# Decoder trunk step on one core: tile 2's h2 rows in their own place, the shift adds on VectorE, and the order of the sample-attention matmuls

## The chip, the cores and the metric

The kernel runs on one core of one Trainium2 chip. The metric is the device time of one launch in microseconds. A core has TensorE (PE, with its weight loads as PEld), VectorE (DVE), ScalarE (ACT), GpSimd (POOL) and SyncE (SP), which here only starts DMAs, and 16 DMA engines that all queues share. Everything is in float32.

## What is computed

One layer for 512 prompt tokens and for 8 samples of 8 tokens each, with the same weights. The samples attend to 2048 past positions whose keys and values lie in pages of the cache.

```
h = rms_norm(x, g_pre_mix) * (1 + sc1) + sh1
z = h @ w_in                        # q, k, v, u, s
a = rms_norm(attend(q, k, v, lam), g_subln) * (1.0 - lam_init)
s_out = spatial_gating(u, vs, sgu_ws, sgu_bs, chunk_len)
mix = concat([a, s_out]) @ w_out
x = x + ga1 * rms_norm(mix, g_post_mix)
h2 = rms_norm(x, g_pre_ffn) * (1 + sc2) + sh2
f = hier_moe(h2)                    # top-1 group of 4, then top-2 of 4 experts
x = x + ga2 * rms_norm(f, g_post_ffn)
```

Each sample's attention reads 2048 keys and 2048 values of 512 numbers each. The mixture of experts has 16 experts, each with three weight matrices of 2 MB.

## The kernel before

The program is a row of stages, each written out by hand for every engine: `condition` and `project` (adaLN and the input projection), `attend_prompt`, `attend_sample`, `merge`, `experts`, `combine`. Inside a stage every engine runs its own list of instructions in the order in which the code issues them, and semaphores tie the lists together. There is no scheduler: what is written first on an engine runs first on it.

The 576 tokens lie in five tiles of rows, t = 0 to 3 with 128 prompt rows each and t = 4 with the 64 sample rows.

**The sample loop (`attend_sample`).** TensorE goes over b = 1 to 8. In pass b it issues `weights` of sample b - 1 (three parts, L1625 and L1632: it turns the softmax weights into columns), `scores` of sample b (L1597), in odd passes `logits` (L1706), then `project_half(b)` (L1679), `values` of sample b - 1 (L1647 and L1652), a turn of the sample's result (`turn_gate` L1721 in pass 1, `turn_o` L1738 after it) and a turn of a prompt tile (`mix_turn` L1663 in odd passes, `x1_turn` L1690 in even ones). `project_half(u)` is one half (512 of 1024 columns) of the prompt's output projection: tile u // 2, column half u % 2, eight matmuls of 128x512 that add up in bank 5 of PSUM. It waits for the turned tile (`mix_ev`), for its half of `w_out` (`wo_in`), and for bank 5 (`half_free`).

The cache pages come through GpSimd's own DMA queue, each sample's keys and values in two loads apiece of 2.1 MB. Keys of sample b + 2 are requested when the scores that used their place are done. Values have one pair of places for all samples but the last: in pass b GpSimd waits for the first half of `values(b - 1)` and requests the first half of sample b's values, then the same for the second:

```
for half in range(2):
    pool.wait_ge(pv_half if half == 0 else pv_done, b)
    self.load_pages(pool, self.cv, b, half, V_SLOT[half])
```

VectorE turns the keys (`turn_block`, L817), adds the position bias and takes the maximum (`bias_max`, L1455), and in even passes from 2 on makes a tile's residual sum x1 (`residual`, L1487, L1494). ScalarE takes the exponential (L1414), copies the results out of PSUM, and empties bank 5 at the start of the next pass (`take_half`, L1339, L1357). SyncE requests the second half of `w_out` at L1253 behind the column rows of the gate.

**The end of the prompt and sample part (`merge`).** VectorE makes h2 of each tile in two instructions, a scale (`h2_scale`, L1932) and the add of the shift (L1938), each over 128x1024. The tiles' rows lie in `hv[t]`. Tile 2 has tile 0's place:

```
hv = [hv0, hv1, hv0, L.at(n0 + 11456, D), L.at(n0 + 9536, D)]
```

so `h2_scale(2)` waits for the store of tile 0 to memory (`h2_out2[0]`). For tiles 2 and 3 VectorE only scales, and GpSimd adds the shift (L1899). SyncE stores the tiles in the order 0, 1, 4, 2, 3 (L1868). The sample rows' own residual and h2 are made in between (L2023, L2024, L2026, L2032; their root mean squares come over ScalarE L1339 and GpSimd L831, L832), then `route(3, 5)` picks the experts of the last two tiles (L1960 to L1981), TensorE counts ranks, and `first` finds the rows of the first expert tile. Its list goes to GpSimd, whose first gather (L2309) waits for it and for all stores of h2. From there on the experts run.

Of the kernel before, what the change touches and what calls it, by code (L numbers as in the profile page):

```python
# [29 lines left out]
NT = 5  # L30
# [188 lines left out]
class Program:  # L219
# [943 lines left out]
    def attend_sample(self, block):  # L1163
# [416 lines left out]
        def _(pe):  # L1580
# [87 lines left out]
            def project_half(u):  # L1668


                t, c = u // 2, u % 2
                pe.wait_ge(mix_ev, 2 * t + 2)
                pe.wait_ge(wo_in[c], 16)
                if u:
                    pe.wait_ge(half_free, u)
                else:
                    pe.wait_ge(own_kept, 1)
                for k in range(KC):
                    last = pe.matmul(PS[:, 5, :], mixT(t)[:, k, :], wo[c][:, k, :], start=k == 0, stop=k == KC - 1)  # L1679
                last.then_inc(half_done, 1)  # L1680
# [60 lines left out]
            for b in range(1, SB + 1):  # L1741
                f, par = b - 1, b % 2
                for part in range(3):
                    weights(f, part, 1 - par)
                if b == 1:
                    project_half(0)
                if b < SB:
                    scores(b, par)
                    if b == SB - 1:
                        pe.wait_ge(at_act, 3 * b)  # L1750
                        pe.wait_ge(wr_made, 2)
                        pe.matmul(PS[:, 4, 32:52], L.cst("ones"), w_sum, start=True, stop=True)
                    if b % 2 and b >= 3:
                        logits((b - 3) // 2)
                    project_half(b)
                values(f)
                if b == 1:
                    turn_gate()
                else:
                    turn_o(b - 2)  # L1760
                if b % 2 and b <= 5:
                    mix_turn((b + 1) // 2, b)
                if b % 2 == 0 and b <= 6:
                    x1_turn((b - 2) // 2)
            self.late_turn = x1_turn, logits, turn_o
# [11 lines left out]
    def merge(self, block):  # L1777
# [19 lines left out]
        hv = [hv0, hv1, hv0, L.at(n0 + 11456, D), L.at(n0 + 9536, D)]  # L1797
# [5 lines left out]
        scales_in, h2_shifted = self.sem("e_scales_in"), self.sem("e_h2_shifted")  # L1803
# [57 lines left out]
        def _(sp):  # L1861

            def store(t):
                if t in (2, 3):
                    sp.wait_ge(h2_shifted, t - 1)
                else:
                    sp.wait_ge(h2_done, (1, 2, 0, 0, 4)[t])
                sp.dma_start(self.h2[P * t:P * t + rows(t), :], hv[t][0:rows(t)]).then_inc(h2_out2[t % 2], 16)  # L1868
# [16 lines left out]
            for t in (0, 1, 4, 2, 3):  # L1885
                store(t)

        @block.gpsimd
        def _(pool):
# [7 lines left out]
            for t in (2, 3):  # L1897
                pool.wait_ge(h2_done, (3, 5)[t - 2])
                pool.tensor_tensor(hv[t], hv[t], shift2, ALU.add).then_inc(h2_shifted, 1)  # L1899
# [24 lines left out]
        def _(dve):  # L1924
            link = chain(dve, dchain, self.dve_count)

            def h2_scale(t, link):

                dve.wait_ge(rs2, t + 1)
                if t == 2:  # L1930
                    dve.wait_ge(h2_out2[0], 16)
                return link(dve.scalar_tensor_tensor(hv[t], self.x1[:, t, :], ss2[:, t:t + 1], scale2,  # L1932
                                                     ALU.mult, ALU.mult))

            def h2_of(t):

                h2_scale(t, link)
# [81 lines left out]
            h2_scale(2, lambda ins: ins.then_inc(h2_done, 1))  # L2019
# [6 lines left out]
            dve.tensor_tensor(x_s, x1, mod_s[1], ALU.mult).then_inc(x1_done, 1)  # L2026
            first(0, 3)
# [5 lines left out]
            h2_scale(3, lambda ins: ins.then_inc(h2_done, 1))  # L2033
# [792 lines left out]
```

## Time and profile before

| What | us |
|---|---|
| median of 3 runs (lowest, highest) | 833.25 (831.74, 834.65) |
| the profiled execution, device time | 834.4 |
| its span in the profile | 832.6 |
| PE busy in the span | 753.8 (91%) |
| DVE, ACT, POOL busy | 362.4, 184.2, 124.1 |
| mean granted clock of TensorE, share of full | 0.948 |

The page's chain of work that ended last gives PE 76%, DVE 8%, DMA 8%, issue 3%. The prompt's attention ends at about 287 us of the span, the sample loop runs from there to 468.7, `merge` to 509, the experts to about 789, `combine` to the end. Times in the rows are microseconds from the start of the span. A square bracket behind a row of the timeline says how long the engine sat idle ahead of it and what ended the idle time; "issue" there means nothing that the profile shows. A matmul of float32 is counted twice, so a group of eight reads x16. The granted clock reads 1.00 at full speed (2.4 GHz) and 0.50 at half (1.2 GHz).

### The profile page before, as it was taken

The page shows a single profiled execution, that of the slowest core. Times are in us where ns is not written, and L with a number is a line of the kernel's source. Part 1 is how long each engine was busy: PE and PEld are TensorE (multiplying, and loading weights), DVE is VectorE, ACT ScalarE, POOL GpSimd, SP SyncE. Part 2 cuts the span into 40 slices and gives each one's busy share as a digit, 9 for nine tenths or more (in the row PEclk, how much of TensorE's full clock was granted, in tenths as well). Part 3 has the DMA queues.
Part 4 walks back from the last instruction along what each step waited for, and adds up shares of the span by engine and source line. Part 5 has one row for each costly group of instructions (what it writes and reads, how often), then busy time and mean ns, then how long its engine had stood idle before and what let it go on. Part 6 is the DMA issues. An engine that isn't in the chain of part 4 may idle for free.

```text
span 832.6 us, 12324 instructions
## 1 busy us (share of the span) xinstructions
PE 753.8 (91%) x5044; PEld 363.4 (44%) x5044; DVE 362.4 (44%) x829; ACT 184.2 (22%) x427; POOL 124.1 (15%) x171
## 2 busy tenths in 40 slices
PE   4699999999999967999999854899999999999994
PEld 3144444444444543555555452444444444444431
DVE  2122343525897965868675768101221010010146
ACT  4001000124455521333333311001111011110132
POOL 2130000200000311323121321100000000000054
PEclk9699999999999988999899965999999999999997
DMA  8989085590000798999999922599999999999893
GB/s 306 407 240 419 26 353 216 155 357 26 13 2 14 286 410 347 375 414 420 408 363 404 317 107 79 197 425 400 414 416 407 426 397 410 412 401 404 372 306 114
DMA packets 36475, 249.01 MB, mean 299 GB/s; under 512 B 4137, under 2 KB 5417, under 8 KB 22978
## 3 DMA queue, kind: packets, MB, share of 16 engines
q1 hardware_dynamic: 26354, 164.49, 50.6%
q0 software_dynamic: 9120, 81.34, 25.1%
q10 hardware_dynamic: 944, 2.38, 0.8%
q8 instruction: 41, 0.67, 0.3%
q14 instruction: 16, 0.13, 0.0%
HBM read 231.79 MB, written 16.40 MB: 298 GB/s over the span
## 4 chain that ended last, share of the span: by engine, by line
PE 76%; DVE 8%; DMA 8%; issue 3%; POOL 2%; ACT 1%; SPq 1%; POOLq 0%; DVEq 0%; ACTq 0%
PE ps L778 10%; PE ps L1679 7%; PE ps L2480 7%; PE ps L2515 7%; PE ps L2490 6%; PE ps L2487 6%; PE ps L1069 5%; PE ps L1597 4%; PE ps L1647 3%; DMA sb<-in_w_ada 3%; PE ps L2520 3%; DMA h_rows<-sb 2%; PE ps L535 2%; PE ps L2452 2%; PE ps L1625 2%
## 5 line engine op out<-in xcount | busy, mean ns | idle before, releaser
L2490 PE MATMUL ps<-sb 128*128 128x512 f32 (+1 forms) x256 | 113.0, 594 | 0.0
L778 PE MATMUL ps<-sb 128*128 128x512 f32 x192 | 87.2, 609 | 1.4 <-DVE sb L436 1.4
L2414 DVE TENSOR_TENSOR sb<-sb,ps 128x512 f32<-128x512 f32 (+1 forms) x16 | 10.9, 683 | 159.9 <-PE ps L2490 79.7
L817 DVE STREAM_TRANSPOSE sb<-sb 128x1024 f32<-128x1024 f32 (+1 forms) x72 | 76.5, 1099 | 6.4 <-DMA sb<-in_cache_k,ints 6.4
L1679 PE MATMUL ps<-sb 128*128 128x512 f32 x128 | 60.8, 630 | 5.0 <-issue 5.0
L2480 PE MATMUL ps<-sb 128*128 128x512 f32 x128 | 60.6, 629 | 4.5 <-DMA sb<-in_w_gate 3.6
L1069 PE MATMUL ps<-sb 128*128 128x512 f32 x128 | 59.2, 597 | 0.3 <-DVE sb L972 0.3
L2487 PE MATMUL ps<-sb 128*64 128x512 f32 x128 | 56.6, 595 | 0.0
L778 PEld LDWEIGHTS ps<-sb 128*128 128x128 f32 x192 | 36.5, 195 | 45.8 <-issue 44.5
L2515 PE MATMUL ps<-sb 128*128 128x512 f32 x128 | 56.5, 594 | 0.0
L2490 PEld LDWEIGHTS ps<-sb 128*128 128x128 f32 (+1 forms) x256 | 41.1, 163 | 30.2 <-issue 30.1
L2309 POOL DMA_INDIRECT sb<-h_rows,ints x16 | 14.8, 928 | 232.2 <-PE ps L2452 206.1
L946 ACT ACTIVATE sb<-sb 128x128 f32<-128x128 f32 (+3 forms) x64 | 35.4, 554 | 53.7 <-DVE sb L1030 53.7
L2425 DVE COPY sb<-ps 128x512 f32<-128x512 f32 (+1 forms) x16 | 11.1, 692 | 70.7 <-PE ps L2515 49.9
L1679 PEld LDWEIGHTS ps<-sb 128*128 128x128 f32 x128 | 25.1, 203 | 37.8 <-issue 37.5
L1030 DVE CUSTOM_DVE_ANT_0 sb<-ps,sb 128x128 f32<-128x128 f32 (+3 forms) x64 | 28.7, 486 | 26.6 <-PE ps L1104 26.5
L2480 PEld LDWEIGHTS ps<-sb 128*128 128x128 f32 x128 | 25.0, 201 | 34.4 <-issue 32.8
L1597 PE MATMUL ps<-sb 32*32 32x512 f32 x1024 | 37.2, 599 | 2.1 <-issue 2.1
L2515 PEld LDWEIGHTS ps<-sb 128*128 128x128 f32 x128 | 23.7, 190 | 26.9 <-issue 26.8
L2343 ACT ACTIVATE sb<-ps 128x512 f32<-128x512 f32 (+1 forms) x16 | 9.5, 595 | 111.4 <-PE ps L2480 59.9
L1069 PEld LDWEIGHTS ps<-sb 128*128 128x128 f32 x128 | 22.9, 193 | 22.0 <-issue 20.9
L2487 PEld LDWEIGHTS ps<-sb 128*64 128x64 f32 x128 | 16.9, 137 | 32.9 <-issue 32.0
(356 smaller groups left out, 1026.0 us busy)
## 6 DMA issues: line engine op xcount, KB each, us to landing
sb<-in_w_gate SPq DMA_DIRECT2D x16, 2048.0 KB, 24.2
sb<-in_w_up SPq DMA_DIRECT2D x16, 2048.0 KB, 14.3
sb<-in_w_down SPq DMA_DIRECT2D x16, 2048.0 KB, 19.0
sb<-in_w_ada SPq DMA_DIRECT2D x12, 2048.0 KB, 18.6
sb<-in_w_in SPq DMA_DIRECT2D x5, 2048.0 KB, 22.3
sb<-in_x_prompt SPq DMA_DIRECT2D x8, 512.0 KB, 8.5
sb<-in_w_out SPq DMA_DIRECT2D x2, 2048.0 KB, 17.1
y_rows<-sb SPq DMA_DIRECT2D x8, 512.0 KB, 19.7
```

The costliest lines, as they stand in the source:

```text
L778: last = pe.matmul(PS[:, n % 4, :], L.hT[:, k, t * P:t * P + P], w[:, k, :], start=k == 0, stop=k == KC - 1)
L817: dve.transpose(block, block).then_inc(self.turned, 1)
L946: act.activation(pb[n % 3][j][:, 0:w], pb[n % 3][j][:, 0:w], ACT.Exp, bias=nm[:, q:q + 1], scale=-1.0, accum_out=sums[:, q:q + 1]).then_in ...
L1030: dve.tensor_tensor_reduce(out=pb[n % 3][j][:, 0:w], in0=PS[:, 2 * (n % 2) + j, 0:w], in1=self.dist_bias[:, h, 384 - P * i:512], scale=-1. ...
L1069: last = pe.matmul(PS[:, bank, :], L.hT[:, k, t * P:t * P + P], w[:, k, :], start=k == 0, stop=k == KC - 1)
L1597: last = pe.matmul(PS[32 * h:32 * h + 32, g, :], qst[par][r, h, 32 * c:32 * c + 32], kp[r, :, at_row:at_row + 32], start=c == 0, stop=c == 3)
L1647: last = pe.matmul(PS[c:c + 32, 7, 0:256], at[:, page, 32 * quad:32 * quad + 32], vp[:, g, 256 * quad:256 * quad + 256], start=page < 2, s ...
L1679: last = pe.matmul(PS[:, 5, :], mixT(t)[:, k, :], wo[c][:, k, :], start=k == 0, stop=k == KC - 1)
L2480: last = pe.matmul(PS[:, 0, :], x[:, k, :], w_gate[:, k, :], start=k == 0, stop=k == KC - 1)
L2487: last = pe.matmul(PS[n:P, 0, :], x[:, k, :], w_gate[:, k, :], start=k == 0, stop=k == KC - 1)
L2490: last = pe.matmul(PS[0:n, 1, :], x[:, k, :], w_up[:, k, :], start=k == 0, stop=k == KC - 1)
L2515: last = pe.matmul(PS[:, 5 + c, :], hT[:, k, :], w[:, k, 512 * c:512 * c + 512], start=k == 0, stop=k == FC - 1)
```

## The change

Four edits. Tile 2's h2 rows get a place of their own, which lies in the area of the sample scores, and the wait for tile 0's store goes. The shift adds of tiles 2 and 3 move from GpSimd to VectorE, right behind their scale; tile 3's pair moves ahead of `first(0, 3)`, where before its scale stood behind the sample rows' h2. SyncE stores the tiles in the order 0 to 4. In the sample loop `values(0)` is issued ahead of `project_half(1)`, and from pass 2 on each `project_half` is issued in two parts: its first four matmuls at the old place, its last four at the end of the pass.

```diff
-            def project_half(u):
+            def project_half(u, blocks=range(KC)):
...
-                for k in range(KC):
+                for k in blocks:
                     last = pe.matmul(PS[:, 5, :], mixT(t)[:, k, :], wo[c][:, k, :], start=k == 0, stop=k == KC - 1)
-                last.then_inc(half_done, 1)
+                if k == KC - 1:
+                    last.then_inc(half_done, 1)
...
                     if b % 2 and b >= 3:
                         logits((b - 3) // 2)
+                    if b > 1:
+                        project_half(b, range(KC // 2))
+                values(f)
+                if b == 1:
                     project_half(b)
-                values(f)
                 if b == 1:
                     turn_gate()
                 else:
...
                 if b % 2 == 0 and b <= 6:
                     x1_turn((b - 2) // 2)
+                if 1 < b < SB:
+                    project_half(b, range(KC // 2, KC))
...
-        hv = [hv0, hv1, hv0, L.at(n0 + 11456, D), L.at(n0 + 9536, D)]
+        hv = [hv0, hv1, L.at(n0 + 2560, D), L.at(n0 + 11456, D), L.at(n0 + 9536, D)]
...
-                if t in (2, 3):
-                    sp.wait_ge(h2_shifted, t - 1)
-                else:
-                    sp.wait_ge(h2_done, (1, 2, 0, 0, 4)[t])
+                sp.wait_ge(h2_done, (1, 2, 3, 4, 5)[t])
...
-            for t in (0, 1, 4, 2, 3):
+            for t in range(NT):
                 store(t)
...
-            for t in (2, 3):
-                pool.wait_ge(h2_done, (3, 5)[t - 2])
-                pool.tensor_tensor(hv[t], hv[t], shift2, ALU.add).then_inc(h2_shifted, 1)
...
-                if t == 2:
-                    dve.wait_ge(h2_out2[0], 16)
-                return link(dve.scalar_tensor_tensor(hv[t], self.x1[:, t, :], ss2[:, t:t + 1], scale2,
-                                                     ALU.mult, ALU.mult))
...
-            h2_scale(2, lambda ins: ins.then_inc(h2_done, 1))
+            h2_of(2)
             finish_logits(3)
...
             dve.tensor_tensor(x_s, x1, mod_s[1], ALU.mult).then_inc(x1_done, 1)
+            h2_of(3)
             first(0, 3)
...
             dve.scalar_tensor_tensor(hv[4][0:NS], x_s, ss2[0:NS, 4:5], mod_s[2], ALU.mult, ALU.add).then_inc(h2_done, 1)
-            h2_scale(3, lambda ins: ins.then_inc(h2_done, 1))
```

On TensorE, passes 1 to 3 of the sample loop. Before, from `scores(1)` to the turn of pass 2 (L1679 is the projection half, L1647 and L1652 are `values`):

```order
L1597 MATMUL ps<-sb 32x512 x64
L1679 MATMUL ps<-sb 128x512 x8
L1647 MATMUL ps<-sb 32x256 x32
L1652 MATMUL ps<-sb 32x256 x2
L1721 MATMUL ps<-sb 128x64 x4
L1663 MATMUL ps<-sb 128x128 x8
L1625 MATMUL ps<-sb 64x64 x32
L1632 MATMUL ps<-sb 64x64
L1597 MATMUL ps<-sb 32x512 x64
L1679 MATMUL ps<-sb 128x512 x8
L1647 MATMUL ps<-sb 32x256 x32
L1652 MATMUL ps<-sb 32x256 x2
```

The same stretch of TensorE's list with the change:

```order
L1597 MATMUL ps<-sb 32x512 x64
L1647 MATMUL ps<-sb 32x256 x32
L1652 MATMUL ps<-sb 32x256 x2
L1679 MATMUL ps<-sb 128x512 x8
L1722 MATMUL ps<-sb 128x64 x4
L1663 MATMUL ps<-sb 128x128 x8
L1625 MATMUL ps<-sb 64x64 x32
L1632 MATMUL ps<-sb 64x64
L1597 MATMUL ps<-sb 32x512 x64
L1679 MATMUL ps<-sb 128x512 x4
L1647 MATMUL ps<-sb 32x256 x32
L1652 MATMUL ps<-sb 32x256 x2
```

In pass 1 the whole projection half now stands behind `values(0)`; in pass 2 only four of its matmuls stand ahead of `values(1)`. The end of pass 2 and the start of pass 3 on TensorE, with the change (`turn_o`, `x1_turn`, the half's second part, `weights`):

```order
L1739 MATMUL ps<-sb 128x64
L1691 MATMUL ps<-sb 128x128 x8
L1679 MATMUL ps<-sb 128x512 x4
L1625 MATMUL ps<-sb 64x64 x32
L1632 MATMUL ps<-sb 64x64
```

The other four matmuls stand behind the turns, directly ahead of the next pass's `weights`, and so on up to pass 7.

On VectorE, in `merge`, from the sum of the sample rows' projection (L2016, L2017) to the first instruction of `route(3, 5)`. Before:

```order
L2017 TENSOR_TENSOR ps<-ps,sb 64x512 [waits dve_chain]
L1932 SCALAR_TENSOR_TENSOR sb<-sb 128x1024 [waits e_h2_out,f_rs2,e_summed]
L1944 SCALAR_TENSOR_TENSOR sb<-sb 128x20 [waits f_log_kept,f_rs2]
L2023 SCALAR_TENSOR_TENSOR sb<-ps,sb 64x1024 [waits f_rs1,dve_chain]
L2024 TENSOR_TENSOR sb<-sb 64x1024 [waits dve_chain]
L2026 TENSOR_TENSOR sb<-sb 64x1024 [waits e_x1]
L1990 SCALAR_TENSOR_TENSOR sb<-ps,sb 128x3 [waits e_rank]
L1992 SCALAR_TENSOR_TENSOR sb<-sb 128x384 [waits dve_chain]
L2029 TENSOR_TENSOR sb<-ps,sb 64x20 [waits f_log]
L2032 SCALAR_TENSOR_TENSOR sb<-sb 64x1024 [waits f_rs2,e_x1]
L1932 SCALAR_TENSOR_TENSOR sb<-sb 128x1024 [waits f_rs2]
L2036 SCALAR_TENSOR_TENSOR sb<-ps,sb 64x20 [waits f_log,e_log_read]
```

From the old L2026 (now L2019) on, with the change:

```order
L2019 TENSOR_TENSOR sb<-sb 64x1024
L1930 SCALAR_TENSOR_TENSOR sb<-sb 128x1024
L1931 TENSOR_TENSOR sb<-sb 128x1024
L1983 SCALAR_TENSOR_TENSOR sb<-ps,sb 128x3
L1985 SCALAR_TENSOR_TENSOR sb<-sb 128x384
L2023 TENSOR_TENSOR sb<-ps,sb 64x20
L2026 SCALAR_TENSOR_TENSOR sb<-sb 64x1024
L2029 SCALAR_TENSOR_TENSOR sb<-ps,sb 64x20
```

Tile 3's scale and add now stand between the sample rows' residual and `first(0, 3)`, and nothing stands between the sample rows' h2 (L2026 there) and the finish of their logits (L2029 there). Tile 2's pair has grown by its add in the same way, at the place of the first L1932.

## Rows read from the trace of the kernel before

**Rows 1.** Timeline of PE, pass 1: start, us, engine, line, operation, tiles, count, [idle before]

```profile
321.25 9.19 PE L1679 MATMUL ps<-sb 128*128 128x512 f32 x16 [5.04 <-issue]
330.37 3.66 PE L1647 MATMUL ps<-sb 128*32 128x256 f32 x64
334.51 0.46 PE L1721 MATMUL ps<-sb 64*128 64x64 f32 x4
```

**Rows 2.** Timeline of PE, pass 2's half, and the first `weights` of pass 3

```profile
342.44 7.21 PE L1679 MATMUL ps<-sb 128*128 128x512 f32 x16
...
355.01 2.08 PE L1625 MATMUL ps<-sb 128*64 128x64 f32 x64
```

**Rows 3.** Busy time by window (columns: PE, PEld, DVE, ACT, POOL, PEclk, DMA share, GB/s)

```profile
321.20:330.40 9.20, 9.15 (x20) 3.79 (x21) 5.02 (x7) 2.15 (x2) 0.00 (x0) 0.77 0.91 385
```

**Rows 4.** Timeline of PE, passes 4 to 6: their first `weights`, and a gap in `scores(5)`

```profile
376.55 2.09 PE L1625 MATMUL ps<-sb 128*64 128x64 f32 x64
...
395.58 2.08 PE L1625 MATMUL ps<-sb 128*64 128x64 f32 x64
...
403.44 1.48 PE L1597 MATMUL ps<-sb 32*32 32x512 f32 x8 [1.34 <-issue]
...
421.79 2.08 PE L1625 MATMUL ps<-sb 128*64 128x64 f32 x64
```

**Rows 5.** DMA: windows 330 to 335 and 385 to 395; the key load issued at 384.74

```profile
DMA packets 28, 0.36 MB, mean 72 GB/s; under 512 B 6, under 2 KB 6, under 8 KB 6
...
DMA packets 285, 4.14 MB, mean 414 GB/s; under 512 B 32, under 2 KB 32, under 8 KB 32
...
sb<-in_cache_k,ints POOLq DMA_INDIRECT x1, 14.6
```

**Rows 6.** Timeline of the loop's end and the start of `merge`, all engines

```profile
461.31 2.09 PE L1625 MATMUL ps<-sb 128*64 128x64 f32 x64
...
464.49 3.66 PE L1647 MATMUL ps<-sb 128*32 128x256 f32 x64 [0.98 <-ACT sb L1405]
...
465.63 1.23 DVE L1938 TENSOR_TENSOR sb<-sb 128x1024 f32<-128x1024 f32 x1
...
468.19 0.34 DVE L1503 SCALAR_TENSOR_TENSOR sb<-sb 64x128 f32<-64x128 f32 x1 [1.34 <-POOL sb L832]
...
468.83 3.65 PE L2145 MATMUL ps<-sb 128*64 128x512 f32 x16
...
475.53 5.35 PE L2145 MATMUL ps<-sb 128*64 128x512 f32 x16 [0.48 <-ACT sb L1383]
```

**Rows 7.** Timeline of DVE and POOL in `merge`, from the sample sum to the last ranks

```profile
481.65 0.69 DVE L2017 TENSOR_TENSOR ps<-ps,sb 64x512 f32<-64x512 f32 x1
...
487.81 1.28 DVE L1932 SCALAR_TENSOR_TENSOR sb<-sb 128x1024 f32<-128x1024 f32 x1 [5.46 <-DMA h_rows<-sb]
...
491.84 1.22 DVE L2026 TENSOR_TENSOR sb<-sb 64x1024 f32<-64x1024 f32 x1
...
493.34 0.78 POOL L832 TENSOR_TENSOR sb<-sb 64x1 f32<-64x1 f32 x1
...
494.24 3.28 DVE L2032 SCALAR_TENSOR_TENSOR sb<-sb 64x1024 f32<-64x1024 f32 x1 [0.43 <-POOL sb L832]
...
498.79 2.34 POOL L1899 TENSOR_TENSOR sb<-sb 128x1024 f32<-128x1024 f32 x1 [2.36 <-DVE sb L1932]
499.10 2.06 DVE L1960 TENSOR_TENSOR sb<-sb 128x8 f32<-128x8 f32 x1
501.19 0.17 DVE L1961 TENSOR_TENSOR sb<-sb 128x8 f32<-128x8 f32 x1
...
505.01 0.19 DVE L1981 TENSOR_TENSOR sb<-sb 128x32 f32<-128x32 f32 x1
```

**Rows 8.** The last store of h2 (issued at 501.2, us to landing) and the first gather

```profile
h_rows<-sb SPq DMA_DIRECT2D x1, 512.0 KB, 2.6
...
509.09 1.02 POOL L2309 DMA_INDIRECT sb<-h_rows,ints  x1 [7.96 <-DVE ints L2061]
```

More of the change, by code:

```diff
@@ L1802, in merge @@
         h2T = L.at(n0 + 18432, KC * NS).rearrange("p (k t) -> p k t", k=KC)
-        scales_in, h2_shifted = self.sem("e_scales_in"), self.sem("e_h2_shifted")
+        scales_in = self.sem("e_scales_in")
         st = self.stats
@@ L1925, in _, with h2_of @@
             link = chain(dve, dchain, self.dve_count)
-            def h2_scale(t, link):
+            def h2_of(t):
                 dve.wait_ge(rs2, t + 1)
-                if t == 2:
-                    dve.wait_ge(h2_out2[0], 16)
-                return link(dve.scalar_tensor_tensor(hv[t], self.x1[:, t, :], ss2[:, t:t + 1], scale2,
-                                                     ALU.mult, ALU.mult))
-            def h2_of(t):
-                h2_scale(t, link)
+                link(dve.scalar_tensor_tensor(hv[t], self.x1[:, t, :], ss2[:, t:t + 1], scale2, ALU.mult, ALU.mult))
                 dve.tensor_tensor(hv[t], hv[t], shift2, ALU.add).then_inc(h2_done, 1)
```

## The prediction

> **What bounds the kernel now.** I read the timeline of TensorE first. It is busy 91% of the span, and in the sample loop almost nothing interrupts it, so what counts there is the few places where it stands. The longest is in pass 1: `scores(1)` ends at 316.2, and the projection half starts at 321.25 after 5.04 us of idle time; it then takes 9.19 us, where the same sixteen counted matmuls take 7.21 us in pass 2 [rows 1, 2]. The window over it shows a granted clock of 0.77 instead of 1.00 [rows 3]. `values(0)`, which needs nothing of the projection, waits behind both. What ends the idle time the profile doesn't name. By the code the half waits there for ScalarE to empty bank 5 and for the second half of `w_out`, requested behind much else; ScalarE is idle by then, so I take the load.
>
> The timelines of all engines over `merge` come second. TensorE is nearly idle there and VectorE carries the chain: it sits 5.46 us until tile 0's rows are stored, because tile 2 wants their place [rows 7]. Then come tile 2's scale, the sample rows' residual, h2, the routing, and GpSimd's first gather at 509.09 [rows 8]. Behind it TensorE and the weight loads start from that gather and from lists that the same VectorE chain makes, so a microsecond won ahead of it is a microsecond of the end. The DMA windows come third. Between 385 and 395 the engines move 4.14 MB, which is two page loads of 2.1 MB, or 5.2 us for one; between 330 and 335 they are nearly idle at 72 GB/s; a key load issued at 384.74 lands 14.6 us later, behind what is queued [rows 5]. A pass needs four such loads, 20.8 us, and a pass of TensorE takes 19 to 21 us. The pages are the next bound, close below.
>
> **The merge part.** Take B as the end of the sample sum (L2017), 482.35, and A as the start of L2026. Before, A is at 491.84, or B + 9.5. The 5.46 us of waiting go. Tile 2's add comes in, one VectorE instruction of 1.23 us by the row of tile 0's add [rows 6, 7]. A is then B + 9.5 - 5.5 + 1.2 = B + 5.2, a gain of 4.2 us. Next late would be the root of the sample rows: ScalarE's square and GpSimd's two operations end near B + 2.1, and VectorE wants them at B + 2.8, so they hide.
>
> From A to the last ranks (L1981, end 505.20) there are 13.4 us before. Three things change. Tile 3's scale and add now stand ahead of `first`, 1.28 + 1.23 = 2.5 us; its scale behind L2032 goes, 1.3 us. Behind L2026 VectorE waited 0.43 us for GpSimd and L2032 took 3.28 us, against 1.22 us for L2026 of the same shape, while GpSimd added tile 2's shift; without that add beside it I take 1.2, so 2.1 + 0.4 go. The first L1960 took 2.06 us beside GpSimd's other add, while the 128x8 instruction behind it takes 0.17: 1.9 us go [rows 7]. That is -2.5 + 1.3 + 2.5 + 1.9 = 3.2 us; 0.4 us of it I don't count, for gaps and for the sample logits, which now come just in time: 2.8 us. GpSimd's root of the sample rows (0.78 us for its last operation) runs under the 2.5 us of tile 3, and the two adds leave GpSimd altogether.
>
> The moved work costs nothing elsewhere. The stores: the last was issued at 501.2 and landed in 2.6 us, 5 us ahead of the gather; now the last is tile 4's, issued some 5 us ahead of where the ranks end, and a gather still comes 3.8 us after those. The merge part gives 4.2 + 2.8 = **7.0 us**. If the cover of the two GpSimd operations is gone, it gives 6.
>
> The Trainium skill, SBUF — State Buffer, section Who interferes with whom, says that a VectorE instruction with two SBUF inputs and a GpSimd one that reads SBUF exclude each other for the whole instruction. By it the sample rows' first root, which now falls under tile 2's pair, would end near B + 3.3 and cost 0.5 us of the 7.0; the same rule is what L2032 at 3.28 us and L1960 at 2.06 us show.
>
> **Pass 1.** With `values(0)` first, TensorE works from 316.2 for the 4.1 us between its first row and the turn behind it [rows 1], to 320.4. The half still can't start before its load is there, 321.25: 0.85 us idle. Then it runs at the full clock, 7.2 instead of 9.2 us. Before, both were done at 334.5; now at 328.5. That is 6.1 us, 4.1 of overlap and 2.0 of clock.
>
> **The split halves.** They add no matmul. Values end 3.6 us earlier in each pass (half of 7.21 [rows 2]), and so GpSimd requests the next sample's value pages 3.6 us earlier, but they are also wanted 3.6 us earlier. Bank 5 is full later, at the end of the pass; ScalarE empties it in 1.4 us while `weights` and `scores` take 6.5, and x1 is wanted much later, so this hides. The scores keep their distance to the `weights` that follow.
>
> What of 6.1 us stays is up to the pages. I ran the queue forward at 5.2 us a load. It starts sample 1's values right behind the keys, which fills the nearly idle 330 to 335 and gains about 5 us on TensorE's 6. By pass 4 the second half of the values lands about 1.9 us after it is wanted. If a gap like the one in pass 5 comes again, TensorE waits no more after that. So the loop gives 6.1 - 1.9 = **4.2 us** up to here, with bounds of 0 (the pages give nothing) and 9 (that gap doesn't come again: pass 5 took 26.2 us from `weights` to `weights` and pass 3, with the same work, 21.5 [rows 2, 4]).
>
> **The loop's end.** At 461.31 TensorE starts the last `weights` and then waits 0.98 us for ScalarE [rows 6], which first took the late result of `values(6)`. Now that result is there 3.6 us earlier, and ScalarE comes 0.4 us sooner. VectorE's sum, tile 0's h2 and the residual of tile 3 also start up to 3 us earlier, and with them the last sample's root. Between its two groups at L2145 TensorE has 3.0 us (472.5 to 475.5), in which it makes two turns and waits for that chain, and the second group takes 5.35 us for what took the first 3.65 us [rows 6]. If the chain is early, some 1.3 us of the 3.0 as waiting and 1.7 us of low clock go. Bounds 0.4 and 3.3; the slower group is as near as the faster one, so I take the middle, **1.9 us**.
>
> **Sum.** 7.0 + 4.2 + 1.9 = 13.1 us. The profiled execution's 834.4 becomes 821.3. It lies 1.15 above the median of 833.25, so the median becomes 820.1; I say **820 us**. A measurement of this kernel tells 0.3%, 2.5 us, from no change.
>
> **Rivals.**
>
> 1. *The loop gives nothing.* The gap at 316.2 is called "issue", as are others in the middle of matmul groups, one of 1.34 us in `scores(5)` where no wait stands in the code [rows 4]. If it is of that kind, or if the pages take all back, only merge and the loop's end pay: 7.0 + 1.9 = 8.9, median 824.4. For it: no releaser named, page queue full. Against it: 5.04 us is far longer than the others, and a wait for a load stands in the code right there. Chance 0.22.
>
> 2. *Everything pays.* The gap of pass 5 doesn't come again and the full clock holds at the loop's end: 7.0 + 9 + 3.3 less 2 for pages, 17.3, median 816. For it: the gap hangs on what is in the DMA queues at that moment, which changes. Chance 0.15.
>
> 3. *Slower: the clock falls in every pass.* TensorE now reaches the values ahead of their pages, waits some 2 us in the middle of a pass, and goes on at half clock. A gap of 1.34 us was enough in pass 5, and that pass cost 4.7 us more than pass 3. Passes 2 to 7 can each lose as much, 28 us, less the 13.1 won: +15, median 848. It decides from the third such pass on (3 x 4.7 = 14 us). Against it: waits of 0.98 us did no harm [rows 6], a slowed pass lets the pages catch up, so that the next pass doesn't wait, and my queue has one or two waits. Chance 0.03. The Trainium skill, TensorE: Matmul & The Clock Gate, section HAM oscillation, describes just this: a DMA wait in each tile throttles the clock in each tile. Pass 5 agrees for one pass; no row shows it in a row of passes.
>
> 4. *The wait for the store isn't gone.* Tile 2's place overlaps the scores, last read by `weights`, long done. Or another wait takes 5 us in its stead. Then the time stays within 3 us of before. Chance 0.03.
>
> The forecast has 0.57. Its own range is 817 to 823.5. To hold 8 in 10 the range takes in most of rival 1 and part of rival 2: **815 to 826**. Faster 0.94, the same 0.03, slower 0.03.
>
> **What would show it.** Right: no wait of VectorE on the store of h2; A to the ranks' end at about 10.6 us; the sample rows' h2 near 1.2 us; the half of pass 1 starting near 321 behind `values(0)` and taking near 7.2; the first gather near 496. Wrong: the gap at 316 now ahead of `values(0)`; waits ahead of `values` in passes 3 to 7 together over 6 us; granted clock under 0.9 over passes 2 to 7; or a gather that waits for a store.

## The result, and the profile after

| What | before | after |
|---|---|---|
| median, us (lowest to highest, runs) | 832.50 (831.48 to 834.65, 4) | 820.02 (819.58 to 825.35, 4) |
| ratio to before (95% interval) | | 0.9864 (0.9826 to 0.9901) |
| profiled execution, device us | 834.4 | 819.93 |
| its span | 832.6 | 818.1 |
| mean granted clock of TensorE | 0.948 | 0.957 |

The change makes the kernel faster, by 1.0% to 1.7% by the interval. The forecast of 820.0 us met the median. That is better than its terms deserve: pass 1 and the loop's end gave more than was booked for them and the pages took back less, and what lay outside the terms took the difference back.

I cut both spans at five marks: the first turn that TensorE issues in the loop (`mix_turn(0)`), B (the end of the sample sum), A (the start of the sample rows' last residual instruction), the end of the last ranks, and the start of the first gather.

| Piece of the span, us | before | after | difference |
|---|---|---|---|
| up to the loop | 287.44 | 288.38 | +0.94 |
| loop start to B | 194.90 | 185.96 | -8.94 |
| B to A | 9.50 | 5.65 | -3.85 |
| A to the ranks | 13.36 | 10.20 | -3.16 |
| ranks to the first gather | 3.89 | 3.88 | -0.01 |
| the rest | 323.51 | 324.03 | +0.52 |
| span | 832.6 | 818.1 | -14.5 |

Pass 1 in the timeline of TensorE after the change (start, us, engine, line, operation, tiles, count, [idle before]):

```profile
313.05 4.46 PE L1597 MATMUL ps<-sb 32*32 32x512 f32 x128
317.44 3.75 PE L1647 MATMUL ps<-sb 128*32 128x256 f32 x64
321.13 0.62 PE L1652 MATMUL ps<-sb 64*32 64x256 f32 x4
322.06 7.10 PE L1679 MATMUL ps<-sb 128*128 128x512 f32 x16 [0.31 <-issue]
329.09 0.46 PE L1722 MATMUL ps<-sb 64*128 64x64 f32 x4
```

`values(0)` (L1647, L1652) now fills the place where TensorE stood, and the half comes 33.68 us after the loop's start, where it came after 33.81 before. So it starts when it did, but finds a running engine, and takes 7.10 us instead of 9.19 [rows 1]. Two rows of the windows of the changed kernel, pass 1 and passes 2 to 7 (columns: PE, PEld, DVE, ACT, POOL, PEclk, DMA share, GB/s):

```profile
316.00:330.00 14.00, 13.69 (x142) 6.48 (x122) 13.79 (x30) 2.91 (x4) 3.76 (x4) 1.00 1.02 416
330.00:456.00 126.00, 122.54 (x1818) 66.03 (x1816) 88.45 (x182) 43.81 (x99) 30.33 (x47) 0.99 1.00 401
```

The granted clock is 1.00 in pass 1 where [rows 3] had 0.77. Over passes 2 to 7 the DMA engines are busy all the time (share 1.00), and the clock holds. The loop's two weak points, from the same timeline of TensorE:

```profile
384.87 1.93 PE L1647 MATMUL ps<-sb 128*32 128x256 f32 x32 [0.70 <-DMA sb<-in_cache_v,ints]
...
399.51 1.06 PE L1597 MATMUL ps<-sb 32*32 32x512 f32 x9 [0.99 <-issue]
400.51 1.86 PE L1707 MATMUL ps<-sb 128*64 128x20 f32 x32
402.30 5.32 PE L1679 MATMUL ps<-sb 128*128 128x512 f32 x8
```

The first is the only wait for value pages. It is in pass 4, on the second half of the values, as the queue worked forward had it, but 0.70 us long instead of 1.9. The second is the old gap in `scores(5)` [rows 4], 0.99 instead of 1.34 us, and again the clock is down behind it: four of a half's matmuls (x8) take 5.32 us, against 3.60 to 3.70 us elsewhere (granted clock 0.69 over them). The loop's end on TensorE and VectorE:

```profile
459.35 3.66 PE L1647 MATMUL ps<-sb 128*32 128x256 f32 x64 [0.69 <-ACT sb L1405]
...
463.70 3.65 PE L2138 MATMUL ps<-sb 128*64 128x512 f32 x16
...
469.13 3.65 PE L2138 MATMUL ps<-sb 128*64 128x512 f32 x16 [0.48 <-ACT sb L1383]
```

Both groups of L2138 now take 3.65 us, where the second took 5.35 [rows 6]. And `merge`, in the timelines of VectorE and GpSimd:

```profile
473.65 0.69 DVE L2010 TENSOR_TENSOR ps<-ps,sb 64x512 f32<-64x512 f32 x1
474.37 1.28 DVE L1930 SCALAR_TENSOR_TENSOR sb<-sb 128x1024 f32<-128x1024 f32 x1
475.69 1.23 DVE L1931 TENSOR_TENSOR sb<-sb 128x1024 f32<-128x1024 f32 x1
475.84 1.49 POOL L832 TENSOR_TENSOR sb<-sb 64x1 f32<-64x1 f32 x1
476.84 0.23 DVE L1937 SCALAR_TENSOR_TENSOR sb<-sb 128x20 f32<-128x20 f32 x1
477.43 1.27 DVE L2016 SCALAR_TENSOR_TENSOR sb<-ps,sb 64x1024 f32<-64x1024 f32 x1 [0.36 <-POOL sb L832]
...
479.99 1.22 DVE L2019 TENSOR_TENSOR sb<-sb 64x1024 f32<-64x1024 f32 x1
...
484.32 1.27 DVE L2026 SCALAR_TENSOR_TENSOR sb<-sb 64x1024 f32<-64x1024 f32 x1
485.97 0.17 DVE L1953 TENSOR_TENSOR sb<-sb 128x8 f32<-128x8 f32 x1
...
490.00 0.19 DVE L1974 TENSOR_TENSOR sb<-sb 128x32 f32<-128x32 f32 x1
494.07 1.02 POOL L2302 DMA_INDIRECT sb<-h_rows,ints  x1 [10.01 <-DVE ints L2054]
```

The 5.46 us ahead of tile 2's scale are gone, the sample rows' h2 (L2026) takes 1.27 instead of 3.28 us, and the first 128x8 instruction of the routing 0.17 instead of 2.06 [rows 7]. The gather still waits for its list (L2054), not for a store. It starts at 494.07, expected near 496.

### The profile page after: what moved, and what is told of

Read it like the earlier page. It is cut to its first block, busy times and chain, and to the rows that moved or that the text cites. A ratio compares the mean times of both kernels' runs of the same rounds, so it can differ in the third digit from the quotient of the medians.

```text
span 818.1 us, 12330 instructions
## 1 busy us (share of the span) xinstructions
PE 750.8 (92%) x5044; PEld 360.6 (44%) x5044; DVE 361.2 (44%) x831; ACT 185.5 (23%) x427; POOL 120.5 (15%) x169
## 4 chain that ended last, share of the span: by engine, by line
PE 74%; DMA 11%; DVE 8%; issue 3%; POOL 2%; ACT 1%; SPq 1%; POOLq 0%; DVEq 0%; ACTq 0%
PE ps L778 10%; PE ps L2473 7%; PE ps L2508 7%; PE ps L2483 6%; PE ps L2480 6%; PE ps L1069 6%; PE ps L1679 5%; DMA sb<-in_cache_v,ints 5%; PE ps L1597 3%; DMA sb<-in_w_ada 3%; PE ps L1647 3%; PE ps L2513 3%; PE ps L535 2%; PE ps L1104 2%; PE ps L2445 2%
## 5 line engine op out<-in xcount | busy, mean ns | idle before, releaser
L1679 PE MATMUL ps<-sb 128*128 128x512 f32 x128 | 60.6, 619 | 0.3 <-issue 0.3
L1679 PEld LDWEIGHTS ps<-sb 128*128 128x128 f32 x128 | 24.0, 198 | 29.1 <-issue 28.8
L1455 DVE CUSTOM_DVE_ANT_1 sb<-ps,sb 128x512 f32<-128x512 f32 x32 | 20.1, 684 | 27.5 <-PE ps L1597 27.5
```

## The experiments

Each is an edit of the kernel before, unless it says that it is one of the changed kernel. The marks (B, A, ranks) are those of the table above; "W7" is the start of the last `weights` (sample 7's), counted from the loop's start. Before has it at 173.87, after at 168.09.

### The merge part alone, and its two halves

`e1_merge_only` is the change without its edits in the sample loop. `e5_place_only` and `e6_adds_only` take it apart.

```diff
# e5_place_only
-        hv = [hv0, hv1, hv0, L.at(n0 + 11456, D), L.at(n0 + 9536, D)]
+        hv = [hv0, hv1, L.at(n0 + 2560, D), L.at(n0 + 11456, D), L.at(n0 + 9536, D)]
...
-                if t == 2:
-                    dve.wait_ge(h2_out2[0], 16)
# e6_adds_only (the stores also go out in the order 0 to 4)
-                pool.wait_ge(h2_done, (3, 5)[t - 2])
-                pool.tensor_tensor(hv[t], hv[t], shift2, ALU.add).then_inc(h2_shifted, 1)
...
-            h2_scale(2, lambda ins: ins.then_inc(h2_done, 1))
+            h2_of(2)
...
+            h2_of(3)
             first(0, 3)
...
-            h2_scale(3, lambda ins: ins.then_inc(h2_done, 1))
```

> The kernel before with the merge part alone: tile 2's own place, the shift adds on VectorE, the stores in order; the sample loop as before. My theory: the wait of 5.46 us for the store goes, the start of L2026 comes 3.9 to 4.2 us sooner after the sample sum, the last ranks another 2.8 to 3.2 us: 7 us in all, ratio 0.9915. Rival (a new wait takes the store's place, or the adds cost VectorE what they free): under 4 us. Rival (merge pays more than its own sum because the chain behind gets earlier too): over 9 us.

> The kernel before with tile 2's own place for its h2 rows and nothing else: GpSimd still adds the shifts of tiles 2 and 3, and tile 3's scale still stands behind the sample rows' h2. Theory: the wait of 5.46 us for tile 0's store goes, but GpSimd's add of tile 2 now falls beside the sample rows' residual on VectorE (two instructions with two SBUF inputs), and its root for those rows queues with the add; L2023 or L2024 takes 2 to 3 us instead of 1.25. The start of L2026 comes 3 to 5.4 us sooner, L2032 near 1.3, and L1960 still near 2 us. Ratio 0.994 to 0.996 (4 to 5 us). Rival: the place is worth all of the merge part, 7 us, ratio 0.9915. Rival: the place is worth under 2 us because GpSimd's add becomes the wait.

> The kernel before with the shift adds on VectorE, tile 3's pair ahead of first(0, 3) and the stores in order, but tile 2 in tile 0's place with its wait for the store. Theory: the 5 us wait stays, A comes 1.2 us later after the sum, and from there to the last ranks it is 3 us shorter: 1.5 to 2 us faster, ratio 0.998. Rival: without the place the adds cost more than they give, ratio 1.000 or over.

| Kernel | median, us (lowest to highest, runs) | ratio (95%) | B to A | A to ranks |
|---|---|---|---|---|
| e1_merge_only | 829.33 (823.54 to 834.0, 12) | 0.9944 (0.9909 to 0.998) | 5.64 | 10.23 |
| e5_place_only | 831.55 (826.62 to 838.88, 12) | 0.9991 (0.9957 to 1.0026) | 4.71 | 13.35 |
| e6_adds_only | 830.02 (826.63 to 838.82, 12) | 0.9984 (0.995 to 1.0018) | 9.87 | 10.20 |

In the pieces the two halves add up to the whole: the place gives 4.8 of B to A, the adds cost up to 0.9 of it and give 3.2 of A to the ranks; together 7.0. In the whole times parts of that size drown. `e1_merge_only` was expected at 0.9915 and came to 0.9944, 4 to 5 us for the 7.0 of its pieces, with the expected ratio just inside its interval; of `e5_place_only` and `e6_adds_only` neither can be told from no change. The trace of `e5_place_only`, whose profiled execution of 838.88 us is the longest of its twelve, shows where the time goes. Timeline of TensorE, its pass 3:

```profile
362.64 1.73 PE L1597 MATMUL ps<-sb 32*32 32x512 f32 x32 [1.72 <-issue]
364.30 3.20 PE L1706 MATMUL ps<-sb 128*64 128x20 f32 x32
367.43 10.04 PE L1679 MATMUL ps<-sb 128*128 128x512 f32 x16
```

A gap of 1.72 us in the middle of `scores(3)`, and behind it the clock is down: pass 3 takes 27.4 us there and 21.5 in the kernel before. Nothing that this edit touches lies near. So executions can differ by more than the 4.8 us of the edit, and the place alone cannot be told from no change by its whole time. I had expected that it could (0.994 to 0.996). Its trace also corrects a smaller point. I had L2021 slowed by GpSimd's add of tile 2 beside it. By the timeline of VectorE it takes its usual 1.28 us, and what it pays is 0.59 us of waiting for GpSimd's root:

```profile
491.03 1.28 DVE L2021 SCALAR_TENSOR_TENSOR sb<-ps,sb 64x1024 f32<-64x1024 f32 x1 [0.59 <-POOL sb L832]
```

### The loop part alone, and its two halves

```diff
# e2_first_only: pass 1's order alone
-                    project_half(b)
+                    if b > 1:
+                        project_half(b)
                 values(f)
+                if b == 1:
+                    project_half(b)
# e3_split_only: the two parts alone
-                    project_half(b)
+                    project_half(b, range(KC // 2) if b > 1 else range(KC))
                 values(f)
...
+                if 1 < b < SB:
+                    project_half(b, range(KC // 2, KC))
```

`e7_loop_only` holds both.

> The kernel before with values(0) ahead of the projection half of pass 1 and nothing else. My theory: the gap of 5 us in pass 1 was for the w_out load, values(0) fills 4.1 us of it and the half then runs at full clock: scores(2) ends 6.1 us sooner, and as no pages are wanted sooner than before relative to their requests, 5 to 6 us arrive at the end: ratio 0.993. Rival (the gap is an instruction gap that now stands ahead of values(0)): no idle time is filled, scores(2) ends at most 2 us sooner, ratio over 0.997. Rival (pages take it back): scores(2) 6 us sooner, last weights under 3 us sooner, and waits on page loads in the trace.

> The kernel before with every projection half from pass 2 on in two parts and nothing else. My theory: passes 2 to 6 keep their length within 0.5 us together, because TensorE has no more and no less to do and pages have some 3 us left; the gain is at the loop's end: the second group of L2138's work at full clock, the chain of the last sample 2 to 3 us sooner: ratio 0.997. Rival (the split costs in each pass): the passes 0.3 us longer each, ratio 0.999 or over. Rival (the split is worth nothing by itself and the loop's end gains through pass 1's edit): ratio 1.000 and L2145's second group still near 5.3 us.

> The kernel before with both edits of the sample loop and the merge as before. Theory: 4 to 5 us in the loop and 2 to 3 us at its end reach only as far as the store's wait: store of tile 0 also goes out sooner, since the expert weights are requested sooner, so 6 to 7 us arrive, ratio 0.992. Rival: the store lands at its old time, for it stands behind the expert weights in SyncE's queue, and the wait in merge grows by what the loop won: under 3 us arrive, wait over 8 us.

| Kernel | median, us (lowest to highest, runs) | ratio (95%) | W7 | W7 to B | B to A |
|---|---|---|---|---|---|
| e2_first_only | 825.44 (823.69 to 828.73, 8) | 0.9912 (0.9881 to 0.9943) | 163.96 | 20.02 | 8.18 |
| e3_split_only | 834.06 (829.49 to 837.51, 12) | 1.0015 (0.9988 to 1.0042) | 175.89 | 17.85 | 8.84 |
| e7_loop_only | 828.24 (823.52 to 831.71, 12) | 0.9937 (0.9908 to 0.9965) | 170.68 | 17.86 | 10.66 |

Pass 1's order alone carries the loop's gain. The split alone shows none in the whole time, though its loop's end is 3.2 us shorter. Its last `weights` came 2.0 us later in the profiled execution, 1.1 us of that by a wait for value pages. It was expected to be faster (0.997) and wasn't.

`e2_first_only` has no split, and its loop's end still came out 1.0 us shorter than before. Timeline of TensorE there:

```profile
454.47 3.66 PE L1647 MATMUL ps<-sb 128*32 128x256 f32 x64 [0.98 <-ACT sb L1405]
...
464.77 0.27 PE L1738 MATMUL ps<-sb 64*128 64x64 f32 x1 [1.20 <-DVE sb L1503]
465.52 3.65 PE L2148 MATMUL ps<-sb 128*64 128x512 f32 x16 [0.48 <-ACT sb L1383]
```

The waits are those of the kernel before, and the second group runs at full clock all the same. The other six traces without a split in pass 7 all have 5.35 us there, and the seven in which part or all of that half stands behind its values all have 3.65 us. So the clock's part of this gain nearly always comes with the moved half, but once came without it.

`e7_loop_only` was expected at 0.992, 6 to 7 us, and came to 0.9937, about 5 us. Two things took back. On the timeline of TensorE, pass 4:

```profile
380.77 1.93 PE L1647 MATMUL ps<-sb 128*32 128x256 f32 x32
385.43 2.87 PE L1647 MATMUL ps<-sb 128*32 128x256 f32 x32 [2.72 <-DMA sb<-in_cache_v,ints]
388.23 1.07 PE L1652 MATMUL ps<-sb 64*32 64x256 f32 x4
...
391.29 4.50 PE L1679 MATMUL ps<-sb 128*128 128x512 f32 x8
```

TensorE waits 2.72 us for the second half of the values. Behind the wait L1652 takes 1.07 us, which takes 0.62 elsewhere, so the clock is down; the pass takes 25.1 instead of 19.0 us. That is rival 3's mechanism, in one pass. Only one more page wait stands in this loop, 0.64 us in pass 2; passes 5 to 7 have none, so the late pages did not go on from pass to pass. The second is VectorE's store wait, in its timeline, and the store that it waits for, issued at 465.5:

```profile
482.12 1.28 DVE L1938 SCALAR_TENSOR_TENSOR sb<-sb 128x1024 f32<-128x1024 f32 x1 [6.62 <-DMA h_rows<-sb]
```

```profile
h_rows<-sb SPq DMA_DIRECT2D x1, 512.0 KB, 16.4
```

The store of 512 KB takes 16.4 us, and SyncE issues it 0.8 us behind a load of a 2 MB weight matrix, with two more such loads still under way; with no load ahead of it, before's last store took 2.6 us [rows 8]. In all six traces in which VectorE waits for this store, it lands 1.1 to 1.4 us behind that load (before: 486.3 and 487.7; here: 480.8 and 481.9). So I read its landing as set by the loads ahead of it. Counted from the loop's start, VectorE got past the wait 5.2 us sooner than before, while the sample sum came 6.4 us sooner. So 1.2 us of what the loop won ended in this wait (B to A is 10.66 instead of 9.50), and only with tile 2's own place does it go through. In the other direction, `e3_split_only` had 8.84 and `e2_first_only` 8.18, so this term moves with the queue from kernel to kernel.

### What the 5.04 us in pass 1 were

`e4_half1_w0` lets the half of pass 1 use the other, long present half of `w_out`, so that nothing has to land for it.

```diff
-                pe.wait_ge(wo_in[c], 16)
+                d = 0 if u == 1 else c
+                pe.wait_ge(wo_in[d], 16)
...
-                    last = pe.matmul(PS[:, 5, :], mixT(t)[:, k, :], wo[c][:, k, :], start=k == 0, stop=k == KC - 1)
+                    last = pe.matmul(PS[:, 5, :], mixT(t)[:, k, :], wo[d][:, k, :], start=k == 0, stop=k == KC - 1)
```

> The kernel before, but the projection half of pass 1 reads the first half of w_out (landed long before) in place of the second, so that it doesn't wait for that load; tile 0's second column half is then computed with the other weights. The amount of work is the same. Theory w_out: the 5 us of idle time ahead of that half go to under 1.5 us (an instruction gap at most), and the half starts near 316.5 to 317.5. Rival instruction gap: the half still starts near 321. Rival bank 5 (ScalarE's copy ends at 313.2): no change either.

Timeline of TensorE, pass 1 of that kernel:

```profile
311.95 4.46 PE L1597 MATMUL ps<-sb 32*32 32x512 f32 x128
316.34 7.13 PE L1680 MATMUL ps<-sb 128*128 128x512 f32 x16
323.41 3.66 PE L1647 MATMUL ps<-sb 128*32 128x256 f32 x64
```

No idle time, and the half at full clock: 7.13 us. The next `weights` (W1) start 41.48 us after the loop's start, against 48.48 before. So the 5.04 us were the wait for the load, though the profile calls them "issue", and both of pass 1's prices, overlap and clock, come from that one wait. This kernel ran once, at 828.46 us, so no ratio is given; its output isn't the layer's, since half of one product uses the other weights. Rival 1, in so far as it made this gap one of the unexplained kind, falls here.

### Do the splits of passes 2 to 6 matter?

Two edits of the changed kernel. `e8_split7` (and the same again, `e10_split7_again`) splits only pass 7's half, `e12_no_split` none. `e9_after_again` is the changed kernel itself, on the same chip as these last two.

```diff
# e8_split7, e10_split7_again
-                        project_half(b, range(KC // 2))
+                        project_half(b, range(KC // 2) if b == SB - 1 else range(KC))
...
-                if 1 < b < SB:
+                if b == SB - 1:
                     project_half(b, range(KC // 2, KC))
# e12_no_split
-                        project_half(b, range(KC // 2))
+                        project_half(b)
...
-                if 1 < b < SB:
-                    project_half(b, range(KC // 2, KC))
```

> The changed kernel with the projection half in two parts in pass 7 only; passes 2 to 6 as before the change. Theory: what the split gives is at the loop's end alone, and in passes 2 to 6 it only brings the values ahead of their pages (0.3 and 0.7 us of waiting in the changed kernel). So this is 0 to 1.5 us faster than the changed kernel: 818.5 to 820. Rival (each pass's split helps, since values free their places sooner): 1 us or more slower than the changed kernel.

> The changed kernel once more, beside e10 on the same chip. Theory: its page waits (pass 1 to 7) are 1 to 3 us together and its time 819 to 822.

> The kernel of e8 once more (projection half in two parts in pass 7 only). Theory: no wait on a page load in the trace, and 1 to 2 us faster than e9 in the median. Rival: the 2 us between the medians of e8 and the changed kernel were scatter of runs, and e9 and e10 agree within 0.5 us.

> The merge part and values(0) first, with no half in two parts at all. Theory: as e10 up to pass 7, and at the loop's end the 3.2 us of the split in pass 7 are missing (from the last weights to the sample sum 20 to 21 us instead of 17.9): 2.5 to 3.5 us slower than e10. Rival (the loop's end is short since pass 1's edit or the merge edits): within 1 us of e10.

| Kernel | median, us (lowest to highest, runs) | ratio (95%) | page waits, us (times) | W7 | W7 to B |
|---|---|---|---|---|---|
| e8_split7 | 817.80 (817.22 to 823.23, 6) | 0.9835 (0.9795 to 0.9876) | none | 166.27 | 17.87 |
| e10_split7_again | 819.34 (816.74 to 824.4, 6) | 0.9841 (0.9796 to 0.9887) | none | 164.98 | 17.87 |
| the change, e9_after_again | 820.27 (818.35 to 821.46, 6) | 0.9842 (0.9802 to 0.9883) | 1.3 (2) | 165.24 | 17.88 |
| e12_no_split | 819.67 (817.26 to 822.48, 6) | 0.9828 (0.9787 to 0.9868) | none | 166.54 | 21.02 |

The traces agree with the mechanism. Without a split in passes 2 to 6 no wait for pages is left, and without the split in pass 7 the loop's end is the old one. Timeline of TensorE, `e12_no_split`:

```profile
457.69 3.66 PE L1647 MATMUL ps<-sb 128*32 128x256 f32 x64 [0.98 <-ACT sb L1405]
...
467.97 0.27 PE L1738 MATMUL ps<-sb 64*128 64x64 f32 x1 [1.19 <-DVE sb L1503]
468.72 5.35 PE L2140 MATMUL ps<-sb 128*64 128x512 f32 x16 [0.48 <-ACT sb L1383]
```

Waits of 0.98 and 1.19 us and a second group at 5.35 us, the same three numbers as in the kernel before ([rows 6] has the first and the last). The whole times do not agree: `e12_no_split` was to be 2.5 to 3.5 us slower than `e10_split7_again` and its median is 0.3 us away; `e10_split7_again` was to beat the change by 1 to 2 us, and the medians are 0.9 us apart (2.2 us for `e8_split7` against the first timing of the change). All four intervals overlap nearly whole. What the runs cannot say is whether the 3.2 us of the loop's end arrive in the median. In the kernel before and in `e1_merge_only`, `e5_place_only` and `e6_adds_only`, whose loops are the same list of instructions, passes 2 to 7 took 125.4, 124.3, 132.2 and 121.8 us, and the stretch behind the first gather, which no kernel here edits, took 323.1 to 327.2 us over all the kernels. Either spread is wider than the term. No version is shown to beat the change.

### Values first in every pass

If it pays in pass 1, why not everywhere? In the changed kernel:

```diff
-                    if b > 1:
-                        project_half(b, range(KC // 2))
                 values(f)
-                if b == 1:
+                if b < SB:
                     project_half(b)
...
-                if 1 < b < SB:
-                    project_half(b, range(KC // 2, KC))
```

> The changed kernel with values ahead of the whole projection half in every pass (no half in two parts), so values end another 3.6 us sooner in a pass. Theory (the page queue paces the loop, one load of 2.1 MB in 5.2 us): TensorE waits for pages in most passes from 2 on, 1 to 4 us each, and a pass takes near 4 x 5.2 = 20.9 us whatever TensorE does; the last weights come 1 to 5 us later than in the changed kernel. Rival (the clock falls in every pass, my forecast's slow case): after each wait the granted clock goes to 0.50 for some us, passes take 24 us and more, the loop ends over 15 us later. Rival (pages have slack): no waits, same time as the changed kernel.

Measured: 832.23 us (830.29 to 835.94, 10 runs), ratio 0.9986 (0.9958 to 1.0013). All that the change had won is gone again. Timeline of TensorE, its passes 2, 2 and 4:

```profile
337.90 0.59 PE L1647 MATMUL ps<-sb 128*32 128x256 f32 x3 [1.10 <-DMA sb<-in_cache_v,ints]
...
342.68 2.48 PE L1647 MATMUL ps<-sb 128*32 128x256 f32 x32 [2.11 <-DMA sb<-in_cache_v,ints]
...
388.52 3.48 PE L1647 MATMUL ps<-sb 128*32 128x256 f32 x32 [2.01 <-DMA sb<-in_cache_v,ints]
```

Its waits by group (engine line waited for: us in total, times, longest) and three windows (columns as above):

```profile
PE ps L1647 <- DMA sb<-in_cache_v,ints: 8.1, 4, 2.9
```

```profile
340.00:350.00 10.00, 7.89 (x53) 3.26 (x47) 9.51 (x15) 2.38 (x3) 3.31 (x3) 0.83 1.00 418
360.00:380.00 20.00, 18.72 (x279) 10.98 (x256) 14.01 (x26) 5.57 (x12) 5.40 (x9) 1.00 0.80 324
380.00:400.00 20.00, 17.82 (x215) 7.68 (x183) 15.29 (x28) 3.65 (x9) 6.47 (x7) 0.91 0.99 413
```

With values first, TensorE reaches each sample's values 7.2 us sooner in a pass than in the kernel before, and their pages are not there: 8.1 us in four waits, two in pass 2 and one each in passes 4 and 6. W7 comes at 179.17, 11 us later than with the change. 7.4 of these 11 are the waits (8.1 less the 0.7 that the change has). The rest I put to the clock, which falls behind some of them (0.83 in the first window, 0.91 in the last; 32 matmuls at 3.48 us that take 1.93). Waiting and hurrying alternate: the DMA share of 0.80 in the middle window says that the queue itself ran dry for a while. I had expected the last `weights` 1 to 5 us later, with waits in most passes; the mechanism was the named one, but the waits came in three of the six passes, and the price was twice its upper end. Among the edits of the loop this is the nearest to rival 3.

## Why the prediction was right

**Merge, 7.0 us: right, its two parts a little off.** Measured 3.85 + 3.16 = 7.0 us; 4.2 + 2.8 was said. B to A came out 0.35 short, since GpSimd's last root operation took 1.49 us beside VectorE's 128x1024 pair and ended at B + 3.0, and VectorE stood 0.36 us for it. I had taken that root as hidden. In `e5_place_only`, where tile 2's pair on VectorE lacks its add, the same operation took 0.54 us. The Trainium skill, SBUF — State Buffer, section Who interferes with whom, was the better guide here: by it the cost was 0.5 us, and 0.36 was measured. (That the one that comes second waits for the whole instruction, the section says of VectorE's modes that use both ports. For two SBUF inputs [rows 7] shows it: L1960 ends at 501.16 us, GpSimd's add beside it at 501.13.) A to the ranks gave 0.36 more than booked: my allowance of 0.4 us for gaps and late logits was not needed.

**Pass 1, 6.1 us: right.** Measured 6.4 us from the loop's start to the next `weights` (48.48 to 42.12). The half's start was the load's landing, as argued from the code against the word "issue"; only 0.31 us of idle time stood there instead of 0.85, and the clock gave 2.1 instead of 2.0. `e4_half1_w0` shows the cause and `e2_first_only` that the gain arrives (ratio 0.9912).

**What the pages take back, 1.9 us: right in place in this execution, too large.** W7 came 5.8 us earlier, so 0.6 of pass 1's 6.4 were lost, and the page wait was 0.70 us. But in `e7_loop_only`, with the same loop, the wait in pass 4 was 2.72 us, and with the clock behind it that pass took 6 us more. And in `e9_after_again`, the same kernel as the change, two waits of 0.6 us stand in passes 2 and 6 and none in pass 4. So one execution's 0.7 is luck, and so is in part the place; 1.9 was a fair middle.

**The loop's end, 1.9 us: too small.** This is the mis-sized term. Measured 3.16 us (21.03 to 17.87 between W7 and B), and 3.1 to 3.2 in every other kernel that moves part of pass 7's half behind its values; without that it is 21.0, but for `e2_first_only` (20.02). Its parts on TensorE are 0.98 - 0.69 = 0.3 for ScalarE, 1.2 for the wait for VectorE, and 5.35 - 3.65 = 1.7 for the clock. I had the bound at 3.3 and took the middle where all three paid together. The first two hang on the one late result, since they change exactly where the half moves. The third need not: `e2_first_only` had it without the other two, where it was worth 1.0 us. So that it came in full each time with the split is shown, and why the clock holds there is not.

**Where the surplus went.** The terms came to 15.95 us instead of 13.1. In the span 1.46 us of it went into the stretches ahead of the loop (+0.94) and behind the gather (+0.52), in which no instruction moved. I read that as scatter between two executions: over all traces here the first stretch takes 286.3 to 290.1 us and the second 323.1 to 327.2. Between the medians the difference is 12.5 us (832.50 to 820.02). So the exact hit is a slightly small sum and a slightly unlucky rest that cancel.

**The rivals.** Rival 1 is refuted by `e4_half1_w0` and `e2_first_only`. Rival 2 half happened (the clock holds at the loop's end), but the gap of pass 5 came again. Rival 3 did not happen: a wait of its size came in one pass of `e7_loop_only`, and three, in passes 2, 4 and 6, in `e11_all_first`, which lost the whole gain and no more. Rival 4 did not happen; `e5_place_only` shows the wait gone in B to A.

## What to carry to other kernels

When an engine stands still for a load, put work there that needs nothing of that load, but read first what that work waits for: the same move gave 6 us in pass 1, where the values' pages had landed, and cost 11 us in passes 2 to 7 when it was made in every pass. A wait for a place in memory is priced by what the store is queued behind (here weight matrices of 2 MB each: 16.4 us for half a MB that takes 2.6 alone), so upstream gains end in it until the place is free. And a term of 3 us in a kernel whose executions scatter by 3 to 12 us is to be read from the pieces of its trace; its median will not show it.

## What was unexpected of the hardware

**The same gap, two clocks.** What a short pause of TensorE costs does not follow from its length. In the middle of `scores(3)`, a gap of 1.69 us left the four matmuls behind it at 3.70 us, their time at full clock (`e3_split_only`, timeline of TensorE):

```profile
361.53 1.44 PE L1597 MATMUL ps<-sb 32*32 32x512 f32 x33 [1.69 <-issue]
...
364.67 3.70 PE L1679 MATMUL ps<-sb 128*128 128x512 f32 x8
```

In `scores(5)` of `e12_no_split`, a gap of 0.56 us was followed by a whole half of 8.78 us instead of 7.13, at a granted clock of 0.81:

```profile
398.22 1.06 PE L1597 MATMUL ps<-sb 32*32 32x512 f32 x8 [0.56 <-issue]
399.21 1.84 PE L1706 MATMUL ps<-sb 128*64 128x20 f32 x32
400.98 8.78 PE L1679 MATMUL ps<-sb 128*128 128x512 f32 x16
```

The rest is as mixed. A gap of 0.57 us in `e2_first_only` and one of 1.55 us in pass 3 of `e12_no_split` left the half at 7.13; one of 0.99 us (the change) put four matmuls at 5.32 instead of 3.70, one of 1.34 us (before) cost its pass 4.7 us, and one of 1.72 us (`e5_place_only`) had the half at 10.04. So the row on which rival 3 rests, pass 5 of the kernel before, is one case of several. What decides is not shown here.

The waits for pages sort better. Behind each of the four of 2.0 us and more (2.72 in `e7_loop_only`; 2.11, 2.01 and 2.91 in `e11_all_first`) the matmuls are slowed, and behind none of the six of 0.64 to 1.13 us. The Trainium skill, TensorE: Matmul & The Clock Gate, section HAM oscillation, describes a clock that is throttled anew behind each DMA wait. `e11_all_first` agrees in part: its granted clock was 0.83 from 340 to 350 us, around the second wait of pass 2, and 0.91 from 380 to 400, around the one of pass 4, but behind its first wait, of 1.10 us, it was still 1.00.

**Gaps that no wait explains.** They stand in the middle of `scores` of passes 3 and 5 and in some traces in the `logits` of pass 7, change their length between executions of nearly the same program (0.72 us in pass 3 before, 1.72 in `e5_place_only`), and are, with the clock behind them, the largest differences between traces that I found. In the kernel before, a packet of the DMA queue that the profile calls "instruction" is moved shortly ahead of both (in 359 to 360 us for the gap that ends at 361.27, in 401 to 402 for the one that ends at 403.44). But there are 15 such packets from 330 to 460 us, and the others have no such gap behind them. Whether they have to do with it was not tried.
